# Forget gate of a two-layer hybrid trunk: the tokens' rows made stationary, the gate's 16 weight columns moving

## The chip, the cores and the metric

The kernel runs on one core of a Trainium2 chip, in one launch. The metric is the device time of that launch in microseconds. The kernel before takes 1617.2 us (median of three runs, 1616.39 to 1618.21).

## The reference, cut to what matters

Two request groups go through two layers with the same weights: one prompt of 512 tokens, and eight samples of 16 tokens with a history of 512. Together these are 640 rows of 1024 channels. A layer norms the rows, multiplies them by `w_in` (columns for retention, forgetting attention and a short convolution), mixes, multiplies by `w_out`, and then runs a gated feed-forward network. Eight columns of `w_in`, `fl`, are the forget gate's logits, one for each of the eight attention heads:

```python
h = _rms_norm(x, norm_mix)
proj = h @ w_in
rq, rk, rv, rg, fq, fk, fv, fl, cb, cc, ch = jnp.split(proj, split_at, axis=-1)
logf = jax.nn.log_sigmoid(fl.astype(f32) + fox_f_bias.astype(f32))
```

Everything is in 32-bit floats. `logf` is an output, and its running sum enters every attention score.

## The kernel before, in words

All 640 tokens are worked on together, as five tiles of 128 (the fifth holds the samples). The normed rows are turned, so that channels lie on partitions: `hhi` and `hlo` have shape [128, 8, 640]. Each float is split in two parts for TensorE's rounded format, the rounded value (`hi`) and the remainder (`lo`). ScalarE writes the first, VectorE the second. Weights come in slabs of 1024 columns per partition (`raw`), and are split in the same way into `whi` and `wlo`. A product is then three matmuls, hi by hi, hi by lo and lo by hi (`mm3`).

Every engine has its own program, written out by hand in the order in which it runs; semaphores join them. PSUM has eight banks; `plan_banks` lists the jobs of each bank in order, and a job waits until the one before it on its bank has been taken out (`wait_room`, `wait_taken`).

In a layer TensorE's order around the gate is this:

- the turning of the normed rows, between the first slabs of chunk 0 (chunk 0: the first 512 columns of `w_in`);
- the rest of chunk 0, then 24 small transposes of the convolution's taps (`rows`);
- the gate's product. Its eight weight columns have a hi and a lo part, side by side in `wfl` [128, 8, 2, 8], 16 columns for each of the eight groups of 128 channels. These 16 columns are the stationary side, and the tokens move, 320 at a time: 2 halves x 8 groups x (`hhi`, `hlo`) = 32 matmuls. The result has 16 rows (8 from the hi weights, 8 from the lo weights) and 640 columns, in two banks. ScalarE takes it to `flr` [16, 640] in two pieces;
- chunk 1, whose tile order is that of `CHUNK_PARTS`, with the turning of the rotated queries and keys (`rt`) in it, and two pieces of chunk 2;
- the gate's turning (`flT`): for each of the five token tiles one matmul with `flr` stationary and a constant `fsum` of eight columns moving. It turns the tile and adds its hi and lo rows. VectorE adds the bias and writes `lf`;
- the retention's scores (`rT`), states (`rv`, `kw`), outputs and, late in that stage, 64 small matmuls of the samples (`qw` by `s0`).

In the rows all matmuls of `mm` stand under L2156 and transposes under L2218, so they are told apart by the names of their tiles.

Of the kernel before, what the change touches and what calls it, by code (L numbers as in the profile page):

```python
# [30 lines left out]
F32 = mybir.dt.float32  # L31
# [3 lines left out]
ALU = mybir.AluOpType  # L35
# [40 lines left out]
CONST = {}  # L76
_at = 0
for _name, _n in (("ident", P), ("tri", 896), ("cs", TT * 64), ("kdec", TT * RH), ("qdec", 2 * P), ("g16", 2),
                  ("tris", P), ("bmask", 16), ("e0", P), ("bsel", NB), ("fsum", FH)):
    CONST[_name] = (_at, _n)  # L80
    _at += _n
NCONST = _at
# [2 lines left out]
def tables():  # L85

    p = np.arange(P)
    gamma = 1.0 - 2.0 ** (-5.0 - np.arange(RH))
    c = np.zeros((P, NCONST), np.float32)

    def put(name, a):
        o, n = CONST[name]
        c[:, o:o + n] = np.asarray(a).reshape(P, n)

    put("ident", np.eye(P))
    pos = np.stack([t * P + p for t in range(TP)] + [PAST + p % NS], 1)
    inv = np.float32(10000.0) ** (-np.arange(HD // 2, dtype=np.float32) / (HD // 2))
    ang = (pos.astype(np.float32)[:, :, None] * inv[None, None, :].astype(np.float32)).astype(np.float64)
    put("cs", np.stack([np.cos(ang), np.sin(ang)], 2))
    left = np.stack([SEQ - 1 - (t * P + p) for t in range(TP)] + [NS - 1 - p % NS], 1)  # L100
    put("kdec", gamma[None, None, :] ** left[:, :, None] * HD ** -0.5)
    par = p // HD
    put("qdec", np.stack([gamma[2 * hp + par][:, None] ** (p[None, :] % NS + 1) for hp in range(2)], 1))
    put("g16", np.stack([gamma[2 * hp + par] ** NS for hp in range(2)], 1))
    put("tri", (np.arange(896)[None, :] - 384) >= p[:, None])
    same = (p[:, None] // NS) == (p[None, :] // NS)
    put("tris", same & (p[:, None] <= p[None, :]))
    b8 = np.arange(NB)
    put("bmask", np.tile((p // NS)[:, None] == b8[None, :], (1, 2)))
    put("e0", (p[:, None] % FH) == (p[None, :] // NS))  # L110
    put("bsel", ((p % HD) // FH)[:, None] == b8[None, :])
    put("fsum", (p[:, None] < 2 * FH) & (p[:, None] % FH == np.arange(FH)[None, :]))

    dp = np.where(p[None, None, :] >= p[:, None, None],
                  gamma[None, :, None] ** np.maximum(p[None, None, :] - p[:, None, None], 0), 0.0)
    i = np.arange(P, SEQ)
    dq = np.stack([gamma[2 * hp + par][:, None] ** (i[None, :] - (SEQ - 1.0)) for hp in range(2)], 1)
    ds = np.where((same & (p[None, :] >= p[:, None]))[:, None, :],
                  gamma[None, :, None] ** np.maximum(p[None, None, :] - p[:, None, None], 0), 0.0)
    decay = np.concatenate([dp.reshape(P, -1) * HD ** -0.5, ds.reshape(P, -1) * HD ** -0.5, dq.reshape(P, -1)], 1)  # L120

    mb = np.zeros((P, P * (2 + NB)), np.float32)
    mb[:, 0:P] = np.eye(P)
    mb[:, P:2 * P] = np.where(p[None, :] <= p[:, None], 0.0, NEG)
    for b in range(NB):
        seen = (p[None, :] // NS == b) & (p[None, :] % NS <= p[:, None] % NS)
        mb[:, (2 + b) * P:(3 + b) * P] = np.where(seen, 0.0, NEG)
    return c, decay.astype(np.float32), mb
# [149 lines left out]
def plan_banks(banks):  # L278

    j = banks.job  # L280
    for t in range(TT):
        for g in range(2):
            j(("hT", 0, t, g), (2 * t + g) % 3)
    cb = chunk_banks()

    def chunk(c):
        for t in range(TT):
            j(("c", c, t), cb[c][t])

    def turns(name):  # L290
        for t in range(TT):
            j((name, t), TURN_BANKS[name][t])

    chunk(0)
    j("taps", 1)
    j(("fl", 0), 0)
    j(("fl", 1), 2)
    chunk(1)
    turns("rt")
    j("flT", 7)  # L300
    for par in range(2):
        j(("rs", 0, par), RET_S[0][par])
    j("rst", 4)
    for par in range(2):
        j(("rs", 1, par), RET_S[1][par])
    for hp in range(2):
        j(("rop", hp), hp)
    for hp in range(2):
        j(("ro", hp), 3 + hp)
    j("rss0", 1)  # L310
    j("rss1", 0)
    j("rds0", 1)
    j("rds1", 0)
    j("rso", 2)
    j("rsoT", 0)
    chunk(2)
    chunk(3)
    turns("qT")
    chunk(4)
    turns("kT")  # L320
    j("cs", 6)
    j("cc", 0)
    j("cn", 5)
    for k, own_banks in (("cc_", (7, 1, 2, 3)), ("ch_", (4, 6, 5, 0)), ("cb_", (2, 3, 2, 2))):
        for i in range(4):
            j((k, i // 2, i % 2), own_banks[i])
    for n, (hp, qbs) in enumerate(fox_units()):
        for par in range(2):
            j(("fs", n, par), FOX_S[n % 2][par])
        if n % 3 == 0 and hp < 3:  # L330
            j(("fo", hp), 1 + hp % 2)
    for n, (hp, qbs) in enumerate(fox_units()):
        for i in range(fox_banks_t(qbs)):
            j(("ft", n, i), FOX_T[i])
    for g in range(3):
        j(("orT", g), (4, 2, 6)[g])
    j(("fo", 3), 5)
    for n in range(STEPS):
        for key, b in batch_jobs(n):
            j(key, b)  # L340
    for n in range(2 * TT):
        j(("wo", n // TT, n % TT), n % 8)
    for t in range(TT):
        for g in range(2):
            j(("hT", 1, t, g), 4 + (2 * t + g) % 4)
    for i in range(4):
        j(("g", "pro", i // 2, i % 2), i)
    for i in range(4):
        j(("u", "pro", i // 2, i % 2), U_BANKS[i])
    banks.loop(PAIRS - 1, wino_jobs("g") + down_jobs() + wino_jobs("u"))  # L350
    for g in range(6):
        j(("last", g), LAST_BANKS[g])
    for key, b in end_jobs():
        j(key, b)
# [7 lines left out]
def build(nc, a):  # L362
    with ExitStack() as ctx:
# [40 lines left out]
        def K(name):  # L404
# [56 lines left out]
            [("upad", [P, 2, PADDED], F32), ("ccs", [P, 2, NTOK], F32)],  # L461
            [("t3h", [P, 4, HALF], F32R), ("t3l", [P, 4, HALF], F32R)],
            [("kbo", [P, 4, FW], F32)],
            [("flr", [2 * FH, NTOK], F32)],
            [("vm", [P, 2, 512], F32)],
            [("gnd", [P, TT * RH, HD], F32), ("gnsq", [P, TT * RH, HD], F32)],
            [("to_gnsq", [P, TT * RH * HD], F32), ("roT", [P, 2, SEQ], F32)],
# [130 lines left out]
        def mark(first, n, key):  # L598
            for s_ in range(first, first + n - 1):
                used_index[s_] = len(used_index)  # L600
            final[first + n - 1] = key

        mark(0, 4, ("c", 0, TT - 1))
        mark(FL, 2, ("fl", 1))
        for c in range(1, 5):
            mark(C0 + 4 * c, 4, ("c", c, TT - 1))
        for first, k in ((CC, "cc_"), (CH, "ch_"), (CB, "cb_")):
# [463 lines left out]
        def _(act):  # L1071
# [92 lines left out]
            for l in range(DEPTH):  # L1164
# [14 lines left out]
                upto(FL + 1, l)  # L1179
                evac("taps", taps[:, :, :], l, view=lambda b: b[:, 0:NCT * NTAP].rearrange("p (c n) -> p c n", c=NCT))  # L1180
                upto(C0 + 4, l)
                for half in range(2):
                    evac(("fl", half), flr[:, half * HALF:(half + 1) * HALF], l, view=lambda b: b[0:2 * FH, 0:HALF])
                upto(C0 + 6, l)

                def silu_tile(t):
# [263 lines left out]
        def _(dve):  # L1450
# [85 lines left out]
            for l in range(DEPTH):  # L1536
# [17 lines left out]
                for t in range(TT):  # L1554
# [22 lines left out]
                    if t in (0, 3):  # L1577
# [3 lines left out]
                upto(C0 + 9, l)  # L1581
                dve.wait_ge(dec_in, l * 48 + 48)
                dve.wait_ge(kw_ready, l * TT + TT)
                B.wait_full(dve, "flT", l)
                dve.wait_ge(foxg_in, l * 64 + 64)
                dve.tensor_tensor(lf[:, :, :], bank[B.bank("flT")][:, 0:40].rearrange("p (t h) -> p t h", t=TT),
                                  fbias[:, :].unsqueeze(1).to_broadcast([P, TT, FH]), ALU.add).then_inc(B.free[B.bank("flT")], 1)
                def masked_values(h):
                    if h == 2:
                        dve.wait_ge(vm_used, l * 2 + 1)  # L1590
# [560 lines left out]
        def _(pe):  # L2151
# [12 lines left out]
            def fill(ins, key):  # L2164

                ins.then_inc(B.full[B.bank(key)], 1)
# [93 lines left out]
            for l in range(DEPTH):  # L2260
# [29 lines left out]

                for i in range(2):
                    ready(FL + i, l)
                for half in range(2):
                    key = ("fl", half)
                    B.wait_room(pe, key, l)
                    ts = slice(half * HALF, half * HALF + HALF)
                    for k in range(KT):
                        for h_ in (hhi, hlo):
                            ins = mm(bank[B.bank(key)][0:2 * FH, 0:HALF], wfl[:, k, :, :].rearrange("p s n -> p (s n)"),
                                     h_[:, k, ts], k == 0 and h_ is hhi, k == KT - 1 and h_ is hlo)  # L2300
                        if half == 1 and k == 3:
                            ins.then_inc(slab_used, 1)
                    fill(ins, key)
                chunk(1, l, "rt", lambda t: pe.wait_ge(rot_ready, l * TT + t + 1))
                for half in range(2):
                    B.wait_taken(pe, ("fl", half), l)
                pieces = iter([(i, t) for i in range(3) for t in range(3)])

                def chunk2(i, tiles, l):
# [5 lines left out]

                for _ in range(2):
                    piece(l)
                B.wait_room(pe, "flT", l)
                for t in range(TT):
                    ins = mm(bank[B.bank("flT")][:, t * FH:(t + 1) * FH], flr[:, t * P:(t + 1) * P], K("fsum")[0:2 * FH, :], True, True)  # L2320
                fill(ins, "flT")


                B.wait_all_taken(pe, [("rt", t) for t in range(TT)] + [("c", 1, t) for t in range(TT)], l)

# [391 lines left out]
```

## Time and profile before

| what | value |
|---|---|
| median of three runs | 1617.2 us |
| profiled execution, device time | 1618.32 us |
| its span, first to last instruction | 1616.5 us |
| TensorE matmuls busy | 1595.0 us, 99% of the span, 10304 records |
| TensorE weight loads busy | 1389.9 us, 86% |
| VectorE busy | 1080.2 us, 67% |
| ScalarE busy | 687.2 us, 43% |
| GpSimd busy | 410.8 us, 25% |
| granted TensorE clock, mean | 0.999 |

The span lies within the device time of the same execution; 1.8 us lie around it. Busy shares are of the whole span. A matmul's recorded duration (some 0.39 us for 512 columns) holds its way through the array; successive ones overlap, so what a stream of them costs is the distance between their starts. A weight load (PEld) is a record of its own and overlaps the matmul ahead. The granted clock is 1.00 at 2.4 GHz and 0.50 at 1.2 GHz.

### The profile page before, as it was taken

The numbers are of one execution on the slowest core, as the hardware profiler recorded it, in microseconds if no ns is written. First come the engines' busy times: TensorE is split into PE (matmuls) and PEld (weight loads), VectorE is DVE, ScalarE is ACT, GpSimd is POOL, SyncE is SP. The second block draws the span as 40 slices with busy tenths as digits, with TensorE's granted clock in tenths as the row PEclk, the third lists the DMA queues.
The fourth block names the chain that finished last, engine by engine and source line by source line (L and its number), as shares of the span: only waits on it lengthen the run. The fifth ranks groups of instructions, "written<-read, shape, count | busy, mean of one in ns | idle before, by whom it ended". The sixth has DMA issues, their size and how long they took to land.

```text
span 1616.5 us, 29200 instructions
## 1 busy us (share of the span) xinstructions
PE 1595.0 (99%) x10304; PEld 1389.9 (86%) x10304; DVE 1080.2 (67%) x1749; ACT 687.2 (43%) x1285; POOL 410.8 (25%) x524
## 2 busy tenths in 40 slices
PE   7999999999999999999999999999999999999998
PEld 6878896688999999999888789867899999999997
DVE  4445447528977777777644553674399777777775
ACT  4224337416544444444433233463264444444442
POOL 1114200004433333333112140010044333333330
PEclk9999999999999999999999999999999999999999
DMA  8223423822222222222242224156213222222222
GB/s 247 79 50 87 137 85 105 301 78 66 79 78 78 85 83 81 90 89 78 72 110 66 70 80 144 66 178 227 85 60 105 85 87 88 78 78 78 78 78 71
DMA packets 125319, 160.04 MB, mean 99 GB/s; under 512 B 25636, under 2 KB 77294, under 8 KB 125166
## 3 DMA queue, kind: packets, MB, share of 16 engines
q1 hardware_dynamic: 125096, 158.65, 32.2%
q8 instruction: 50, 0.82, 0.2%
q10 hardware_dynamic: 144, 0.33, 0.1%
q14 instruction: 29, 0.24, 0.0%
HBM read 149.43 MB, written 9.53 MB: 98 GB/s over the span
## 4 chain that ended last, share of the span: by engine, by line
PE 94%; DVE 2%; ACT 1%; DVEq 1%; issue 1%; DMA 1%; POOL 0%; POOLq 0%; SPq 0%; ACTq 0%
PE bank L2156 89%; PE bank L2218 5%; DVEq L1837 1%; DVE pf L1840 1%; DMA raw<-in_w_in 0%; DVE xn L1505 0%; ACT pf L1284 0%; DMA raw<-in_w_gate 0%; DVE small L1827 0%; DVE hlo L1484 0%; DVE gulo L1484 0%; ACT xn L1152 0%; POOL small L923 0%; ACT hhi L1130 0%; POOLq L1046 0%
## 5 line engine op out<-in xcount | busy, mean ns | idle before, releaser
L2156 PE MATMUL bank<-whi,hhi 128*128 128x512 f32 x560 | 226.7, 405 | 2.4 <-ACT rso L1171 1.1
L2156 PE MATMUL bank<-whi,hlo 128*128 128x512 f32 x560 | 220.2, 393 | 0.0
L2156 PE MATMUL bank<-wlo,hhi 128*128 128x512 f32 x560 | 219.8, 393 | 0.0
L2156 PE MATMUL bank<-hhi,whi 128*128 128x320 f32 x640 | 199.2, 311 | 0.8 <-DVE hlo L1484 0.8
L2156 PE MATMUL bank<-hlo,whi 128*128 128x320 f32 x640 | 198.1, 310 | 0.0
L2156 PE MATMUL bank<-hhi,wlo 128*128 128x320 f32 x640 | 198.0, 309 | 0.0
L2156 PE MATMUL bank<-whi,guhi 128*128 128x512 f32 x440 | 174.1, 396 | 0.4 <-DVE gulo L1484 0.4
L2156 PE MATMUL bank<-wlo,guhi 128*128 128x512 f32 x440 | 173.8, 395 | 0.0
L2156 PE MATMUL bank<-whi,gulo 128*128 128x512 f32 x440 | 173.7, 395 | 0.0
L1460 DVE TENSOR_TENSOR wlo<-raw,whi 128x1024 fp32r<-128x1024 f32 x80 | 100.1, 1252 | 106.1 <-ACT whi L1079 104.8
L1943 DVE TENSOR_TENSOR x<-x,bank 128x512 f32<-128x512 f32 x220 | 143.1, 682 | 39.6 <-PE bank L2156 39.3
L2156 PEld LDWEIGHTS bank<-whi,hhi 128*128 128x128 f32 x560 | 106.1, 190 | 27.2 <-issue 4.6
L2156 PEld LDWEIGHTS bank<-whi,hlo 128*128 128x128 f32 x560 | 106.0, 189 | 23.1
L1079 ACT ACTIVATE whi<-raw 128x1024 fp32r<-128x1024 f32 x80 | 84.6, 1060 | 92.7 <-PE bank L2156 84.4
L2156 PEld LDWEIGHTS bank<-wlo,hhi 128*128 128x128 f32 x560 | 106.5, 190 | 19.9
L2156 PEld LDWEIGHTS bank<-hhi,whi 128*128 128x128 f32 x640 | 120.3, 188 | 2.5 <-issue 1.6
L2156 PEld LDWEIGHTS bank<-hlo,whi 128*128 128x128 f32 x640 | 120.3, 188 | 0.9
L2156 PEld LDWEIGHTS bank<-hhi,wlo 128*128 128x128 f32 x640 | 120.2, 188 | 0.0
L1044 POOL TENSOR_TENSOR s<-raw 128x512 f32<-128x512 f32 x60 | 90.1, 1502 | 83.6 <-DMA raw<-in_w_gate 83.6
L1044 POOL TENSOR_TENSOR s<-raw,gains 128x512 f32<-128x512 f32 x20 | 27.7, 1385 | 317.8 <-DMA raw<-in_w_up 227.7
L2156 PEld LDWEIGHTS bank<-whi,gulo 128*128 128x128 f32 x440 | 82.9, 188 | 19.3
L2156 PEld LDWEIGHTS bank<-whi,guhi 128*128 128x128 f32 x440 | 82.9, 188 | 19.3 <-DVE gulo L1484 1.0
(312 smaller groups left out, 3662.1 us busy)
## 6 DMA issues: line engine op xcount, KB each, us to landing
raw<-in_w_in SPq DMA_DIRECT2D x52, 512.0 KB, 3.7
raw<-in_w_gate SPq DMA_DIRECT2D x44, 512.0 KB, 3.8
raw<-in_w_down SPq DMA_DIRECT2D x44, 512.0 KB, 3.7
vb<-in_cache_fox_v SPq DMA_DIRECT2D x16, 1024.0 KB, 6.8
raw<-in_w_up SPq DMA_DIRECT2D x24, 512.0 KB, 3.8
gains<-in_w_up SPq DMA_DIRECT2D x20, 512.0 KB, 3.8
raw<-in_w_out SPq DMA_DIRECT2D x16, 512.0 KB, 4.8
kb<-in_cache_fox_k SPq DMA_DIRECT2D x8, 1024.0 KB, 6.7
```

The source lines that it names most:

```text
L1044: pool.tensor_tensor(by_k(out[:, :]), x_, y_, op).then_inc(s_sum, 1)
L1079: act.activation(whi[:, slot(n), 0:width(n)], raw[:, slot(n), 0:width(n)], ACT.Copy).then_inc(hi_split, 1)
L1460: dve.tensor_tensor(wlo[:, s_, 0:w_], raw[:, s_, 0:w_], whi[:, s_, 0:w_].bitcast(F32), ALU.subtract).then_inc(lo_split, 1)
L1837: dve.drain()
L1840: ins = dve.tensor_scalar(pf[:, m % 3, par, o:o + N], pf[:, m % 3, par, o:o + N], col(REC + fox_stat(m, i, par)), None, ALU.mult)
L1943: dve.tensor_tensor(x[:, t, 512 * c:512 * c + 512], x[:, t, 512 * c:512 * c + 512], bank[B.bank(key)][:, :], ALU.add).then_inc(B.free[B.ba ...
L2156: return pe.matmul(out, lhsT=lhsT, rhs=rhs, start=start, stop=stop, skip_group_check=True)
L2218: ins = pe.transpose(dst, src, ident[0:src.shape[0], 0:src.shape[0]])
```

## The change

The two sides of the gate's product are swapped. For each token tile, 128 tokens of `hhi` or `hlo` are stationary and the 16 columns of `wfl` move: 5 tiles x 8 groups x (`hhi`, `hlo`) = 80 matmuls. The result has the tokens on partitions, 5 x 16 columns in one bank. ScalarE takes it out in one piece. The five turning matmuls, their wait for both halves, their bank job and the constant `fsum` go; VectorE adds the hi and lo columns and then the bias.

```diff
-    j(("fl", 0), 0)
-    j(("fl", 1), 2)
+    j("fl", 0)
     chunk(1)
     turns("rt")
-    j("flT", 7)
...
-            [("flr", [2 * FH, NTOK], F32)],
+            [("flr", [P, TT, 2 * FH], F32)],
...
                 upto(C0 + 4, l)
-                for half in range(2):
-                    evac(("fl", half), flr[:, half * HALF:(half + 1) * HALF], l, view=lambda b: b[0:2 * FH, 0:HALF])
+                evac("fl", flr[:, :, :], l, view=lambda b: b[:, 0:TT * 2 * FH].rearrange("p (t n) -> p t n", t=TT))
                 upto(C0 + 6, l)
...
-                B.wait_full(dve, "flT", l)
+                B.wait_taken(dve, "fl", l)
                 dve.wait_ge(foxg_in, l * 64 + 64)
-                dve.tensor_tensor(lf[:, :, :], bank[B.bank("flT")][:, 0:40].rearrange("p (t h) -> p t h", t=TT),
-                                  fbias[:, :].unsqueeze(1).to_broadcast([P, TT, FH]), ALU.add).then_inc(B.free[B.bank("flT")], 1)
+                dve.tensor_tensor(lf[:, :, :], flr[:, :, 0:FH], flr[:, :, FH:], ALU.add)
+                dve.drain()
+                dve.tensor_tensor(lf[:, :, :], lf[:, :, :], fbias[:, :].unsqueeze(1).to_broadcast([P, TT, FH]), ALU.add)
...
-                for half in range(2):
-                    key = ("fl", half)
-                    B.wait_room(pe, key, l)
-                    ts = slice(half * HALF, half * HALF + HALF)
+                B.wait_room(pe, "fl", l)
+                for t in range(TT):
+                    ts = slice(t * P, (t + 1) * P)
                     for k in range(KT):
                         for h_ in (hhi, hlo):
-                            ins = mm(bank[B.bank(key)][0:2 * FH, 0:HALF], wfl[:, k, :, :].rearrange("p s n -> p (s n)"),
-                                     h_[:, k, ts], k == 0 and h_ is hhi, k == KT - 1 and h_ is hlo)
-                        if half == 1 and k == 3:
+                            ins = mm(bank[B.bank("fl")][:, t * 2 * FH:(t + 1) * 2 * FH], h_[:, k, ts],
+                                     wfl[:, k, :, :].rearrange("p s n -> p (s n)"), k == 0 and h_ is hhi, k == KT - 1 and h_ is hlo)
+                        if t == TT - 1 and k == 3:
                             ins.then_inc(slab_used, 1)
-                    fill(ins, key)
+                fill(ins, "fl")
                 chunk(1, l, "rt", lambda t: pe.wait_ge(rot_ready, l * TT + t + 1))
-                for half in range(2):
-                    B.wait_taken(pe, ("fl", half), l)
...
-                B.wait_room(pe, "flT", l)
-                for t in range(TT):
-                    ins = mm(bank[B.bank("flT")][:, t * FH:(t + 1) * FH], flr[:, t * P:(t + 1) * P], K("fsum")[0:2 * FH, :], True, True)
-                fill(ins, "flT")
```

On TensorE, in the first layer, from the taps' transposes to chunk 1: each row is a matmul, its bank, its moving and its stationary tile, and the shape of its result; the rows between are 28 more of the same pair, 14 into bank 0 and 14 into bank 2. Before:

```order
L2218 MATMUL bank1<-const_50,rows_116 128x19 x24
L2156 MATMUL bank0<-hhi_56,wfl_82 16x320
L2156 MATMUL bank0<-hlo_57,wfl_82 16x320
...
L2156 MATMUL bank2<-hhi_56,wfl_82 16x320
L2156 MATMUL bank2<-hlo_57,wfl_82 16x320
L2156 MATMUL bank1<-whi_53,hhi_56 128x512
```

And now, with 78 more of the pair's rows where the dots are:

```order
L2215 MATMUL bank1<-const_50,rows_116 128x19 x24
L2153 MATMUL bank0<-wfl_82,hhi_56 128x16
L2153 MATMUL bank0<-wfl_82,hlo_57 128x16
...
L2153 MATMUL bank1<-whi_53,hhi_56 128x512
L2153 MATMUL bank1<-wlo_54,hhi_56 128x512
```

Nothing else moved into or out of this place: the 32 matmuls have become 80, each with a 128-column weight load in place of a 16-column one, and chunk 1 follows as it did. The second place is behind the two pieces of chunk 2, ahead of the retention's scores. Before:

```order
L2156 MATMUL bank6<-wlo_54,hhi_56 128x512
L2156 MATMUL bank6<-whi_53,hlo_57 128x512
L2156 MATMUL bank7<-const_50,flr_139 128x8 x5
L2156 MATMUL bank0<-rT_97 128x128
L2156 MATMUL bank1<-rT_97 128x128
```

Now:

```order
L2153 MATMUL bank6<-whi_53,hhi_56 128x512
L2153 MATMUL bank6<-wlo_54,hhi_56 128x512
L2153 MATMUL bank6<-whi_53,hlo_57 128x512
L2153 MATMUL bank0<-rT_97 128x128
L2153 MATMUL bank1<-rT_97 128x128
```

The scores now follow chunk 2's pieces directly. On ScalarE, at the first place, what stands between the splits of the weight slabs (`whi`), before and then now:

```order
L1171 ACTIVATE taps<-bank 128x456
L1079 ACTIVATE whi<-raw 128x1024
L1171 ACTIVATE flr<-bank 16x320 x2
L1079 ACTIVATE whi<-raw 128x1024 x2
L1171 ACTIVATE rT<-bank 128x4x128
```

```order
L1168 ACTIVATE taps<-bank 128x456
L1076 ACTIVATE whi<-raw 128x1024
L1168 ACTIVATE flr<-bank 128x80
L1076 ACTIVATE whi<-raw 128x1024 x2
L1168 ACTIVATE rT<-bank 128x4x128
```

Two evacuations have become one; the two splits behind it still wait for it.

## Rows read from the trace of the kernel before

**Rows 1.** The page's chain that ended last: shares of the span by engine.

```profile
PE 94%; DVE 2%; ACT 1%; DVEq 1%; issue 1%; DMA 1%; POOL 0%; POOLq 0%; SPq 0%; ACTq 0%
```

**Rows 2.** TensorE's waits: who waited, for whom, us in total, times, longest.

```profile
PE bank L2218 <- DVE xn L1505: 11.0, 5, 9.1
PE bank L2156 <- DVE hlo L1484: 1.9, 3, 1.0
PE bank L2156 <- ACT rso L1171: 1.1, 2, 0.6
```

**Rows 3.** Timeline, TensorE, layer 1: start us, length us, stationary size, moving size, count.

```profile
45.83 1.65 PE L2218 MATMUL bank<-const,rows 19*128 19x19 f32 x24
47.41 0.32 PE L2156 MATMUL bank<-hhi,wfl 128*16 128x320 f32 x1
...
51.97 0.31 PE L2156 MATMUL bank<-hlo,wfl 128*16 128x320 f32 x1
52.12 0.40 PE L2156 MATMUL bank<-whi,hhi 128*128 128x512 f32 x1
```

**Rows 4.** The same, gate's turning, weight loads and matmuls.

```profile
84.58 1.19 PEld L2156 LDWEIGHTS bank<-const,flr 16*128 16x128 f32 x10 [0.35 <-issue]
84.58 1.28 PE L2156 MATMUL bank<-const,flr 16*128 16x8 f32 x10
85.79 1.16 PE L2156 MATMUL bank<-rT 64*128 64x128 f32 x16
```

**Rows 5.** Weight loads of tile flr, both layers: duration ns min/median/max.

```profile
L2156 PEld LDWEIGHTS bank<-const,flr x20: 180/187/188, 84.6 to 885.9; 16*128 16x128 f32 x20
```

**Rows 6.** Timeline, weight loads of 128 columns close behind each other.

```profile
189.78 0.19 PEld L2156 LDWEIGHTS bank<-tri,lcdl 128*128 128x128 f32 x1
189.89 0.30 PEld L2156 LDWEIGHTS bank<-const,lexp 128*128 128x128 f32 x2
190.11 0.19 PEld L2156 LDWEIGHTS bank<-hhi,whi 128*128 128x128 f32 x1
190.22 0.19 PEld L2156 LDWEIGHTS bank<-hlo,whi 128*128 128x128 f32 x1
```

**Rows 7.** Timeline, TensorE, layer 1, late retention stage.

```profile
108.82 2.04 PE L2156 MATMUL bank<-qw,s 64*64 64x16 f32 x64
111.44 0.47 PE L2156 MATMUL bank<-whi,hhi 128*128 128x512 f32 x1 [0.57 <-ACT rso L1171]
...
114.72 0.63 PE L2156 MATMUL bank<-whi,hlo 128*128 128x512 f32 x1
115.15 0.63 PE L2156 MATMUL bank<-whi,hhi 128*128 128x512 f32 x1
...
115.85 0.39 PE L2156 MATMUL bank<-whi,hlo 128*128 128x512 f32 x1
```

**Rows 8.** Windows: length, busy us (count) of PE PEld DVE ACT POOL, granted clock, DMA.

```profile
111.00:112.00 1.00, 0.56 (x3) 0.50 (x4) 1.00 (x2) 0.29 (x1) 0.00 (x0) 1.00 0.00 0
112.00:113.00 1.00, 1.00 (x4) 0.79 (x3) 0.86 (x2) 0.00 (x0) 0.00 (x0) 0.62 0.00 0
115.00:116.00 1.00, 1.00 (x4) 0.76 (x4) 1.00 (x2) 0.00 (x0) 0.00 (x0) 0.67 1.01 174
908.00:912.00 4.00, 3.43 (x77) 2.69 (x74) 0.74 (x2) 0.38 (x1) 0.00 (x0) 1.00 0.02 4
912.00:914.00 2.00, 2.00 (x11) 1.60 (x11) 1.86 (x4) 0.00 (x0) 0.00 (x0) 1.00 0.00 0
```

**Rows 9.** Timeline, TensorE, the program's start.

```profile
9.11 1.94 PE L2218 MATMUL bank<-const,xn 128*128 128x128 f32 x8 [9.11 <-DVE xn L1505]
12.09 0.79 PE L2156 MATMUL bank<-whi,hhi 128*128 128x512 f32 x1 [1.04 <-DVE hlo L1484]
...
16.52 0.47 PE L2156 MATMUL bank<-wlo,hhi 128*128 128x512 f32 x1
...
17.06 1.03 PE L2218 MATMUL bank<-const,xn 128*128 128x128 f32 x8
```

**Rows 10.** Timeline, ScalarE and VectorE around the gate, layer 1.

```profile
52.32 0.43 ACT L1171 ACTIVATE flr<-bank 16x320 f32<-16x320 f32 x1 [1.92 <-PE bank L2156]
52.65 1.99 ACT L1079 ACTIVATE whi<-raw 128x1024 fp32r<-128x1024 f32 x2
...
86.06 0.20 DVE L1586 TENSOR_TENSOR lf<-bank,fbias 128x40 f32<-128x40 f32 x1 [5.89 <-PE bank L2156]
```

More of the change, by code:

```diff
@@ L78 @@
 for _name, _n in (("ident", P), ("tri", 896), ("cs", TT * 64), ("kdec", TT * RH), ("qdec", 2 * P), ("g16", 2),
-                  ("tris", P), ("bmask", 16), ("e0", P), ("bsel", NB), ("fsum", FH)):
+                  ("tris", P), ("bmask", 16), ("e0", P), ("bsel", NB)):
     CONST[_name] = (_at, _n)
@@ L111, in tables @@
     put("bsel", ((p % HD) // FH)[:, None] == b8[None, :])
-    put("fsum", (p[:, None] < 2 * FH) & (p[:, None] % FH == np.arange(FH)[None, :]))
     dp = np.where(p[None, None, :] >= p[:, None, None],
@@ L603, in build @@
         mark(0, 4, ("c", 0, TT - 1))
-        mark(FL, 2, ("fl", 1))
+        mark(FL, 2, "fl")
         for c in range(1, 5):
```

## The prediction

> **What bounds the kernel now.** I began with the chain of waits: 94% of it is TensorE [rows 1]. TensorE's own list of waits then shows how little slack it has: 9.1 us before its first instruction, and after that only a few waits of a microsecond or less [rows 2]. So a microsecond added to TensorE's stream is a microsecond of the kernel, wherever it stands, and one taken away from it comes back. The timeline gives the two places that the change touches: the gate's product from 47.41 to 52.12 us [rows 3] and the gate's turning from 84.58 to 85.79 us [rows 4]. The second layer repeats both.
>
> **The stream as it is.** 32 matmuls of 320 columns start in 52.12 - 47.41 = 4.71 us, 0.147 us each [rows 3]. Their 16-column weight loads are hidden.
>
> **The stream as it will be.** 80 matmuls move 16 columns each, but each needs a load of 128 columns. No row shows just this pair. The nearest one is the turning that goes away: 128-column loads with 8 columns moving. Ten loads span 1.19 us, the last is 0.187 us long [rows 4, 5], so they start (1.19 - 0.187)/9 = 0.111 us apart; the ten matmuls, by the same sum without a row for the last one's length, come to about 0.114. Loads in the rounded format also start 0.11 us apart where the matmul between them is short [rows 6]. Upper bound: the whole turning over its ten loads, 1.21/10 = 0.121 us. Lower bound: the taps' transposes, whose loads are 128 columns wide as well and which take (47.41 - 45.83)/24 = 0.066 us each [rows 3]; they are transposes of 19 rows, an unlike operation, and I keep them for a rival. I take 0.1125 us: 80 x 0.1125 = 9.0 us, so +4.3 us a layer at the full clock (3.9 at 0.1075, 5.0 at 0.121).
>
> The Trainium skill, "TensorE: Matmul & The Clock Gate", section "Weight-path perf modes", says that fast weight load is given to 128-column weights unless they are FP32. By it no load here gets faster, and the sum stands; if the rule did not hold for the rounded format, the transposes' price would be the better one.
>
> **What goes.** The turning, from 84.58 to the next block's start at 85.79: -1.2 us a layer [rows 4]. The 0.35 us of issue ahead of it I count as staying, since the scores that now follow the 512-column matmuls need the same kind of change to a part of the array. Swapping ends there: +4.3 - 1.2 = +3.1 us a layer.
>
> **Edits that I cost at nothing.** ScalarE's one evacuation in place of two (0.43 us each, [rows 10]) starts when the product is full. The next tile on its bank is chunk 1's second, 6 matmuls or about 1.4 us behind; an evacuation of 80 columns started about 0.2 us after the product leaves that uncovered by nothing. Were it late, TensorE would wait for the rest of its 0.4 us. The two slab splits behind it started 0.5 us after the product's end and take 1.99 us; the slab that they feed first is wanted after 18 matmuls, 4.1 us, with one more pass of VectorE between: the distance is what it was. VectorE's extra add of 0.20 us falls in the 5.89 us for which it sat idle before `lf` [rows 10]; its wait is now met long before. Behind it stands the retention's masking, which waits for TensorE's scores in any case. No DMA and no queue is passed.
>
> **The clock.** This is the term that decides the size. The granted clock falls once in the whole trace, and it falls behind the one long run of matmuls that move just 16 columns: 64 of them from 108.82 us, a wait of 0.57 us, three full matmuls, then 0.62 in the window from 112 and back to 1.00 in the one from 115 [rows 7, 8]. In that time 512-column matmuls start 0.43 us apart (114.72 to 115.15) where they otherwise start 0.23 apart, which is the 1.2 GHz level. In the second layer the same sequence shows 1.00 throughout [rows 8], so that run was only just enough. The new product is also a run of 16-column matmuls, 9.0 us and not 2.0, and the taps' 1.6 us of 19-column transposes stand directly ahead of it. I expect the clock to fall inside it in both layers.
>
> What a weight load costs at the lower level can be read at the program's start, where matmuls are half as fast though the record of the clock shows no fall: eight transposes take 1.94 us there and 1.03 us at 17.06 [rows 9]. So I double the distance, to 0.22 us (0.212 by the ratio 0.43/0.227 of the big matmuls). In layer 1 of the trace the small run began at 108.82 and the clock fell at about 112.2, 3.4 us on. At 0.1125 us that is 30 of the new loads at full clock, and 50 at half: 50 x 0.1075 = +5.4 us. Then the lower level stays for a while: from 112.2 to 115.6 in [rows 7, 8], and through 4.4 us of dense work at the start, 12.09 to 16.52 [rows 9]. 3.4 us at half speed lose 1.7 us (4.4 would lose 2.2; a return soon after the product 0.4). Together +7.1 us a layer.
>
> Against this stands a rule. The Trainium skill, same page, section "HAM oscillation", ties the fall to gaps in which TensorE idles between bursts. By it the gapless product would keep its clock, and the kernel would be at the first rival's time. This trace does not agree in full: its fall has a gap of only 0.57 us in it.
>
> **The sum.** Per layer +4.3 - 1.2 + 5.4 + 1.7 = +10.2 us; two layers +20.4. The profiled execution's 1618.3 us would become 1638.7. It stands 1.1 above the median of the runs, so against the median: 1617.2 + 20.4 = 1637.6 us. Bounds of this case: 40 to 70 loads at half clock (4.3 to 7.5), 0.4 to 2.2 after, and one fall behind the `qw` run more or less (1.7 us in all): 1617.2 + 2 x (3.1 + 4.7) - 1.7 = 1631 to 1617.2 + 2 x (3.1 + 9.7) + 1.7 = 1645.
>
> **The rivals.**
> - *The clock holds.* Weight loads of the whole array may keep the level up, where the `qw` run's loads were 64 by 64; the second layer's `qw` run kept it, and so did the turning and the scores at 84.58. Then only the swap counts: 2 x 3.1 = 6.2 us, 1623.4 us (1622.6 to 1624.8 by the bounds of the load). Against it: the one fall there is, behind a shorter run.
> - *It falls in one layer only*, as with `qw`: 10.2 + 3.1, 1630.5 us.
> - *Not slower: the loads run at the taps' pace.* If a 128-column load with a narrow moving side starts every 0.066 us, the product takes 5.3 us, +0.6 - 1.2 = -0.6 us a layer, 1616.0 us in all. The product and the turning together are 4.71 + 1.21 = 5.92 us, so it decides below 5.92/80 = 0.074 us. For it: 24 rows of taps. Against it: ten of `flr` and the rounded format's loads at 0.11. By the skill's rule on FP32 it would not happen either.
> - *The whole product at half clock.* If the taps' transposes pull the clock down before the product begins: 80 x 0.1075 = 8.6, and 2.2 after, 3.1 + 10.8 = 13.9 a layer: 1645 us. The taps alone did not do it before.
>
> **How the numbers follow.** Falls in both layers 0.68, in one 0.08, clock holds 0.16, taps' pace 0.05, all at half clock 0.03. Forecast 1637.6 us. The range goes down to the second case, since without it more than 2 in 10 would be out: 1623 to 1645 us. A measurement of this kernel tells 0.2%, 3.2 us, from no change. Slower by more than that are all cases but the taps' pace: 0.93. Same: 0.05. Faster, 0.02, would need that pace and a saving in the turning's changeover too.
>
> **What would show it.** 160 matmuls `bank<-wfl,hhi` and `bank<-wfl,hlo`, 128*128 stationary and 128x16 moving, start 0.11 us apart at first and 0.21 to 0.22 from some point on; the granted clock shows about 0.50 from 2 to 5 us into the product until some microseconds into chunk 1; chunk 1 begins 4.3 us later than now if the clock holds, near 10 us later if it falls. The retention's scores follow 0.3 us behind chunk 2's matmuls, and VectorE no longer waits before `lf`. I am wrong if the clock stays at 1.00 through the product, if the distance at full clock is under 0.10 us, or if TensorE shows a new wait at chunk 1's second tile.

## The result, and the profile after

The changed kernel takes 1638.28 us (median of four runs, 1637.87 to 1641.84) against 1617.03 us for the kernel before (four runs; the 1617.2 us above are the median of its first three). The ratio is 1.0135, 95% interval 1.0123 to 1.0147. The forecast was 1637.6 us. The profiled execution took 1638.27 us with a span of 1636.5 us, 20.0 us more than before. In its rows all matmuls stand under L2153 and transposes under L2215.

The gate's product in the first layer, timeline of TensorE (start us, length us); it answers to [rows 3]:

```profile
45.32 1.66 PE L2215 MATMUL bank<-const,rows 19*128 19x19 f32 x24
46.91 0.28 PE L2153 MATMUL bank<-wfl,hhi 128*128 128x16 f32 x1
47.04 0.26 PE L2153 MATMUL bank<-wfl,hlo 128*128 128x16 f32 x1
...
50.06 0.26 PE L2153 MATMUL bank<-wfl,hhi 128*128 128x16 f32 x1
50.17 0.30 PE L2153 MATMUL bank<-wfl,hlo 128*128 128x16 f32 x1
50.32 0.36 PE L2153 MATMUL bank<-wfl,hhi 128*128 128x16 f32 x1
50.53 0.36 PE L2153 MATMUL bank<-wfl,hlo 128*128 128x16 f32 x1
...
60.77 0.36 PE L2153 MATMUL bank<-wfl,hlo 128*128 128x16 f32 x1
60.99 0.77 PE L2153 MATMUL bank<-whi,hhi 128*128 128x512 f32 x1
```

Up to 50.17 the starts are (50.06 - 47.04)/27 = 0.112 us apart, from 50.32 on (60.77 - 50.53)/48 = 0.213. The 80 matmuls take 60.99 - 46.91 = 14.08 us where the 32 took 4.71.

The second layer, the same view:

```profile
855.09 0.28 PE L2153 MATMUL bank<-wfl,hhi 128*128 128x16 f32 x1
...
855.67 0.26 PE L2153 MATMUL bank<-wfl,hlo 128*128 128x16 f32 x1
855.78 0.36 PE L2153 MATMUL bank<-wfl,hhi 128*128 128x16 f32 x1
855.99 0.36 PE L2153 MATMUL bank<-wfl,hlo 128*128 128x16 f32 x1
...
871.57 0.77 PE L2153 MATMUL bank<-whi,hhi 128*128 128x512 f32 x1
```

Here only six start at the short distance, and the product takes 16.48 us. The windows over both stretches (length, busy us and count of PE, PEld, DVE, ACT, POOL, granted clock, DMA share, GB/s):

```profile
46.90:50.30 3.40, 3.40 (x32) 3.39 (x31) 1.23 (x1) 1.50 (x2) 0.00 (x0) 0.99 0.02 5
50.30:61.00 10.70, 10.70 (x53) 10.70 (x52) 0.00 (x0) 0.00 (x0) 0.00 (x0) 0.50 0.17 49
61.00:63.80 2.80, 2.80 (x8) 2.22 (x9) 1.41 (x2) 2.13 (x3) 0.00 (x0) 0.50 0.00 0
855.10:855.80 0.70, 0.70 (x8) 0.70 (x7) 0.00 (x0) 0.60 (x2) 0.00 (x0) 0.99 0.00 0
855.80:871.50 15.70, 15.70 (x76) 15.70 (x76) 1.22 (x1) 0.89 (x1) 0.00 (x0) 0.50 0.12 34
871.60:876.20 4.60, 4.60 (x12) 3.63 (x13) 3.04 (x6) 2.13 (x3) 0.00 (x0) 0.50 0.15 26
117.00:122.00 5.00, 4.42 (x83) 3.59 (x80) 1.90 (x3) 0.38 (x1) 0.00 (x0) 1.00 0.00 0
```

The clock is at 0.50 from 50.3 to 63.8 us and from 855.8 to 876.2 us, 2.8 and 4.6 us into chunk 1. In both stretches PE and PEld are busy all the time: no gap precedes the fall. Busy here means that some matmul's record is open; it doesn't mean that columns move all the time. The last row is the stretch with the 64 small `qw` matmuls: the one fall that the kernel before had there [rows 8] is not in this execution.

The second place, TensorE, answers to [rows 4]: the turning is gone, and the scores start 0.36 us behind the last matmul of chunk 2's pieces.

```profile
94.48 0.39 PE L2153 MATMUL bank<-whi,hlo 128*128 128x512 f32 x1
94.84 1.16 PE L2153 MATMUL bank<-rT 64*128 64x128 f32 x16
```

ScalarE and VectorE, answering to [rows 10]; one evacuation of 0.24 us, and no wait of VectorE ahead of `lf`:

```profile
61.17 0.24 ACT L1168 ACTIVATE flr<-bank 128x80 f32<-128x80 f32 x1 [12.66 <-PE bank L2153]
```

```profile
90.33 0.19 DVE L1582 TENSOR_TENSOR lf<-flr 128x40 f32<-128x40 f32 x1
```

TensorE's waits are those of [rows 2], with nothing new among them:

```profile
PE bank L2215 <- DVE xn L1501: 10.4, 5, 8.7
PE bank L2153 <- DVE hlo L1480: 1.8, 3, 0.8
PE bank L2153 <- ACT rso L1168: 1.1, 2, 0.6
```

### The profile page after: what moved, and what is told of

Read it like the earlier page. It is cut to its first block, busy times and chain, and to the rows that moved or that the text cites. A ratio compares the mean times of both kernels' runs of the same rounds, so it can differ in the third digit from the quotient of the medians.

```text
span 1636.5 us, 29396 instructions
## 1 busy us (share of the span) xinstructions
PE 1615.8 (99%) x10380; PEld 1412.9 (86%) x10380; DVE 1081.2 (66%) x1751; ACT 685.1 (42%) x1283; POOL 410.2 (25%) x524
## 4 chain that ended last, share of the span: by engine, by line
PE 93%; DVE 3%; ACT 1%; DVEq 1%; DMA 1%; issue 1%; POOL 0%; POOLq 0%; SPq 0%; ACTq 0%
PE bank L2153 88%; PE bank L2215 5%; DVE pf L1837 1%; DVEq L1834 1%; DMA raw<-in_w_gate 0%; DMA raw<-in_w_in 0%; DVE xn L1501 0%; DVE hlo L1480 0%; ACT pf L1280 0%; DVE x L1940 0%; POOLq L1043 0%; POOL s L1041 0%; DVE small L1824 0%; DVE gulo L1480 0%; DVE wlo L1470 0%
## 5 line engine op out<-in xcount | busy, mean ns | idle before, releaser
L2153 PE MATMUL bank<-whi,hhi 128*128 128x512 f32 x560 | 227.2, 406 | 2.2 <-ACT rso L1168 1.1
L2153 PE MATMUL bank<-whi,hlo 128*128 128x512 f32 x560 | 220.6, 394 | 0.0
L2153 PE MATMUL bank<-wlo,hhi 128*128 128x512 f32 x560 | 220.5, 394 | 0.0
L2153 PE MATMUL bank<-hhi,whi 128*128 128x320 f32 x640 | 198.9, 311 | 1.0 <-DVE hlo L1480 1.0
L2153 PE MATMUL bank<-hlo,whi 128*128 128x320 f32 x640 | 197.8, 309 | 0.0
L2153 PE MATMUL bank<-hhi,wlo 128*128 128x320 f32 x640 | 197.7, 309 | 0.0
L2153 PE MATMUL bank<-whi,guhi 128*128 128x512 f32 x440 | 174.0, 395 | 0.4 <-DVE gulo L1480 0.4
L2153 PE MATMUL bank<-wlo,guhi 128*128 128x512 f32 x440 | 173.6, 395 | 0.0
L2153 PE MATMUL bank<-whi,gulo 128*128 128x512 f32 x440 | 173.6, 395 | 0.0
L2153 PEld LDWEIGHTS bank<-whi,hhi 128*128 128x128 f32 x560 | 106.7, 191 | 27.2 <-issue 4.6
L2153 PEld LDWEIGHTS bank<-whi,hlo 128*128 128x128 f32 x560 | 106.5, 190 | 23.2
L2153 PEld LDWEIGHTS bank<-wlo,hhi 128*128 128x128 f32 x560 | 106.9, 191 | 20.3
L2153 PEld LDWEIGHTS bank<-hhi,whi 128*128 128x128 f32 x640 | 120.1, 188 | 2.6 <-issue 1.8
L2153 PEld LDWEIGHTS bank<-hlo,whi 128*128 128x128 f32 x640 | 120.2, 188 | 0.9
L2153 PEld LDWEIGHTS bank<-hhi,wlo 128*128 128x128 f32 x640 | 120.1, 188 | 0.0
L2153 PEld LDWEIGHTS bank<-whi,gulo 128*128 128x128 f32 x440 | 82.8, 188 | 19.4
L2153 PEld LDWEIGHTS bank<-whi,guhi 128*128 128x128 f32 x440 | 82.8, 188 | 19.4 <-DVE gulo L1480 1.0
```

What stands on the lines that cost most here:

```text
L2153: return pe.matmul(out, lhsT=lhsT, rhs=rhs, start=start, stop=stop, skip_group_check=True)
```

## The experiments

All times are medians. Kernels e1 to e4 ran on one chip, where the kernel before takes 1617.08 us; e5 to e7 ran later on another, where it takes 1616.50 us. The ratios are against the kernel before on the same chip.

**e1: 128 columns move.**

```diff
-                            ins = mm(bank[B.bank("fl")][:, t * 2 * FH:(t + 1) * 2 * FH], h_[:, k, ts],
-                                     wfl[:, k, :, :].rearrange("p s n -> p (s n)"), ...)
+                            ins = mm(bank[B.bank("fl")][:, (t % 4) * P:(t % 4) * P + P], h_[:, k, ts],
+                                     wfl[:, :, :, :].rearrange("p k s n -> p (k s n)"), ...)
```

> The changed kernel, but each of the 80 matmuls moves all 128 columns of wfl in place of 16 (the gate's logits are then not computed; that part is left out). Theory A: the 128-column weight load sets the pace, and the clock fell because the product moves only 16 columns a matmul. 128 columns at full clock need 53 ns, less than the load's 0.111 us, so the distance stays at 0.11 us; the granted clock stays at 1.00; per layer 80 x 0.1115 = 8.9, less 4.7, less 1.2 for the turning: +3.0, in all 1617.0 + 6.0 = 1623 us. Theory B: a stream of back-to-back weight loads brings the clock down whatever moves: the clock falls as in the changed kernel, 1638 us. Theory C: the matmul, not the load, sets the pace: the distance grows by up to 47 ns, 80 x 0.047 x 2 = 7.5 us more than A, 1630 us.

Measured: 1637.48 us, ratio 1.0092 (1.0059 to 1.0125). The medians alone give 1.0126; the runs lie too far apart for either figure to say much. Five executions took 1639.18, 1621.8, 1637.48, 1638.06 and 1630.08 us, with a mean clock of 0.99, 1.0, 0.99, 0.99 and 0.995. TensorE in the profiled one (1639.18 us), first layer:

```profile
50.59 0.28 PE L2153 MATMUL bank<-wfl,hlo 128*128 128x128 f32 x1
50.71 0.31 PE L2153 MATMUL bank<-wfl,hhi 128*128 128x128 f32 x1
50.82 0.41 PE L2153 MATMUL bank<-wfl,hlo 128*128 128x128 f32 x1
51.03 0.42 PE L2153 MATMUL bank<-wfl,hhi 128*128 128x128 f32 x1
```

The distance is 0.11 us ahead of the fall (50.59 to 50.71), with eight times as much moving: the number of columns does not set it, and theory C falls. The clock fell all the same, so theory A, that it was the 16 columns, fails as I put it; theory B's 1638 us fits three of five executions, but not the one at 1621.8 us, whose mean clock was 1.0, nor the one at 1630.08 us. The first is the case "the clock holds" (A's 1623 us), and the second lies where a fall in one layer was put. The same kernel shows all three.

**e5: 256 columns move.** The same edit with `h_[:, k, 0:256]` as the moving side, made after e1's result.

> As e1_wide, but each of the 80 matmuls moves 256 columns of hhi or hlo (the gate's logits are left out). In the rows of before 256-column matmuls of this format start 0.115 us apart, as long as a weight load. Theory A': how much moves behind each load decides whether the clock holds; 16 columns lose it, 128 lose it mostly, 256 keep it: granted clock 1.00 in both layers, 80 x 0.115 = 9.2, less 4.7, less 1.2: 1617.0 + 6.6 = 1623.6 us. Rival B': back-to-back loads of 128 four-byte columns lose the clock whatever moves: 1638 us or more.

Measured: 1624.12 us (1623.48 to 1624.72), ratio 1.0046 (1.0031 to 1.0061). The windows over the product, first layer and second:

```profile
48.00:58.00 10.00, 10.00 (x86) 9.97 (x86) 1.23 (x1) 1.50 (x2) 0.00 (x0) 1.00 0.19 54
850.00:870.00 20.00, 20.00 (x133) 18.27 (x133) 9.17 (x16) 3.63 (x5) 2.14 (x2) 1.00 0.28 79
```

The 80 matmuls and their weight loads start 0.120 us apart (48.45 to 57.80 is 78 distances), nearly as dense as the 0.112 us of the changed kernel, and the clock holds in both layers. The product takes 9.7 us in each, +3.8 us a layer with the turning gone, which is the 7.6 us above the kernel before; 0.115 us a matmul had been expected. So dense loads alone do not take the clock down (rival B' falls), and the kernel that moves sixteen times as much is 14 us faster. With 16 columns the clock fell in both layers of the profiled execution and the four runs lie together; with 128 it fell mostly, with 256 in none of three. I draw no threshold from three points.

**e2: the product spread over chunk 0's last slab.**

```diff
-                chunk0(3, l)
-                ... the taps' transposes
                 for t in range(TT):
+                    chunk0(3, l, [t])
                     ... the 16 gate matmuls of token tile t
+                ... the taps' transposes
```

> The changed kernel, with the product's five token tiles (16 matmuls, 1.8 us each) placed one behind each token tile of chunk 0's last slab (6 matmuls of 512 columns, 1.4 us), so no instruction more or less. Theory A: it is the long unbroken run of 16-column matmuls that loses the clock; broken up by 512-column ones the clock holds, and only the weight loads remain: 1623 us. Rival: runs of 1.8 us are as long as the qw run of 2.0 us behind which the clock fell once in the kernel before, so it falls in some of them: 1625 to 1638 us.

Besides what is expected there, the taps' transposes change places with the product and now stand behind its last piece.

Measured: 1634.56 us, ratio 1.0109 (1.0094 to 1.0124), inside the rival's range but only in part for the rival's reason. TensorE in the first layer, the first gate tile with its neighbours, and what follows the last:

```profile
40.31 0.40 PE L2153 MATMUL bank<-whi,hlo 128*128 128x512 f32 x1
40.54 0.17 PE L2153 MATMUL bank<-wfl,hhi 128*128 128x16 f32 x1
40.57 0.26 PE L2153 MATMUL bank<-wfl,hlo 128*128 128x16 f32 x1
...
42.13 0.26 PE L2153 MATMUL bank<-wfl,hlo 128*128 128x16 f32 x1
42.24 0.48 PE L2153 MATMUL bank<-whi,hhi 128*128 128x512 f32 x1
42.56 0.39 PE L2153 MATMUL bank<-wlo,hhi 128*128 128x512 f32 x1
...
54.99 1.66 PE L2215 MATMUL bank<-const,rows 19*128 19x19 f32 x24
59.50 0.79 PE L2153 MATMUL bank<-whi,hhi 128*128 128x512 f32 x1 [2.85 <-DVE wlo L1456]
```

```profile
39.00:57.00 18.00, 17.58 (x134) 16.20 (x134) 0.00 (x0) 0.31 (x1) 0.00 (x0) 1.00 0.11 30
57.00:59.50 2.50, 0.00 (x0) 0.00 (x0) 1.28 (x2) 2.50 (x5) 0.00 (x0) 0.68 0.00 0
```

And in the second layer, timeline and windows:

```profile
862.69 0.26 PE L2153 MATMUL bank<-wfl,hlo 128*128 128x16 f32 x1
862.88 2.35 PE L2215 MATMUL bank<-const,rows 19*128 19x19 f32 x24
868.07 0.79 PE L2153 MATMUL bank<-whi,hhi 128*128 128x512 f32 x1 [2.85 <-DVE wlo L1456]
```

```profile
849.00:863.40 14.40, 14.40 (x109) 13.34 (x108) 0.00 (x0) 0.00 (x0) 0.00 (x0) 1.00 0.07 25
863.50:865.20 1.70, 1.70 (x17) 1.61 (x16) 0.00 (x0) 0.00 (x0) 0.00 (x0) 0.50 0.00 0
```

In both layers the whole product ran at 1.00. But moving it ahead of chunk 0's end took away what had covered the split of chunk 1's first slab: TensorE now waited 2.85 us for `wlo` in each layer, 5.7 us in all. The clock fell behind the product in both. In the first layer it fell inside the wait, which begins at 56.65. In the second it fell between 863.4 and 863.5, ahead of the wait and without a gap, some 0.6 us into the transposes, which took 2.35 us in place of 1.66. So the wait is not the whole cause: the last 16 gate matmuls and the 24 transposes now stand back to back, 3.4 us of narrow work. The wait was unforeseen and spoiled the time, but this execution shows that the product in pieces of 16, parted by 512-column matmuls, ran at 1.00.

**e6: the same, with the wait mended.** The taps' transposes go behind the first tile, and the 80 matmuls are cut 18, 19, 19, 24 behind the other four. So the transposes no longer touch a piece of the product.

```diff
-                chunk0(3, l)
+                chunk0(3, l, [0])
                 ... the taps' transposes
-                for t in range(TT):
-                    ... the 16 gate matmuls of token tile t
+                for t, n in ((1, 18), (2, 19), (3, 19), (4, 24)):
+                    chunk0(3, l, [t])
+                    ins = gate(n)
```

> As e2_spread, with its new wait mended: the taps' transposes stand behind the first tile of chunk 0's last slab, the 80 gate matmuls in pieces of 18, 19, 19 and 24 behind the other four tiles, so that no run of them is longer than 2.7 us and the last one covers the split of chunk 1's first slab. Nothing is left out. Theory A: the clock holds in both layers and TensorE shows no wait for wlo; only weight loads and the turning count, 80 x 0.1115 = 8.9, plus 0.1 for each of four changes to 512 columns, less 4.7, less 1.2: 1617.0 + 6.6 = 1623.6 us. Rival: a run of 2.7 us is enough for a fall, in one layer or both: 1626 to 1632 us.

Measured: 1622.36 us (1621.81 to 1623.97), ratio 1.0037 (1.0024 to 1.005); the expected terms add up to +6.8 us, not the +6.6 written. TensorE's waits name `wlo` no longer. The windows over the product, first layer and second:

```profile
38.00:60.00 22.00, 22.00 (x155) 19.65 (x154) 3.64 (x5) 3.97 (x6) 0.00 (x0) 1.00 0.21 65
845.00:870.00 25.00, 25.00 (x152) 22.16 (x151) 9.17 (x16) 3.19 (x4) 2.13 (x2) 1.00 0.22 64
```

The same 80 matmuls, the same results, the same evacuation, and 5.9 us above the kernel before on its chip, where the changed kernel was 21.3 us above its own runs of before: some 15 us are what the clock cost, and 5.9 us what the swap costs at full clock. Theory A holds for this order of work. Two things differ from the changed kernel, though: the long run is broken up, and the transposes no longer touch it. In all four kernels that lost the clock at this place (the changed one, e1, e2, e4) they do; in e5 they do as well, and it held. No run has 80 matmuls in one piece without the transposes beside them, so how much of the fall is theirs is not shown.

**e3: the turning alone.** The kernel before without the five turning matmuls; `lf` is made from a constant.

```diff
-                B.wait_room(pe, "flT", l)
-                for t in range(TT):
-                    ins = mm(bank[B.bank("flT")][:, t * FH:(t + 1) * FH], ...)
-                fill(ins, "flT")
...
-                B.wait_full(dve, "flT", l)
-                dve.tensor_tensor(lf[:, :, :], bank[B.bank("flT")][:, 0:40]...
+                dve.tensor_tensor(lf[:, :, :], K("cs")[:, 0:40]...
```

> The kernel before without the five turning matmuls a layer, VectorE adds the bias to a constant (the gate's logits are left out). It shows the second part of the change alone. By the prediction's term: -1.2 us a layer, 1617.0 - 2.4 = 1614.6 us. Rival: the retention's scores then come so early that they wait for ScalarE's evacuations of chunk 1, and nothing comes back: 1617.0 us.

Measured: 1615.02 us, ratio 0.9991 (0.9982 to 1.0), which is 2.1 us less than the median of before; the ratio's interval runs from no effect to 2.9 us. The timeline of TensorE settles what the times leave wide: the scores start 0.35 us behind the last 512-column matmul, with no wait for ScalarE.

```profile
83.53 0.39 PE L2154 MATMUL bank<-whi,hlo 128*128 128x512 f32 x1
83.88 1.16 PE L2154 MATMUL bank<-rT 64*128 64x128 f32 x16
```

**e4: two-byte weights.**

```diff
+                pe.wait_ge(masks_in, 16)
...
-                            ins = mm(bank[B.bank("fl")][:, t * 2 * FH:(t + 1) * 2 * FH], h_[:, k, ts],
-                                     wfl[:, k, :, :].rearrange("p s n -> p (s n)"), ...)
+                            ins = mm(bank[B.bank("fl")][:, t * 2 * FH:(t + 1) * 2 * FH], identb,
+                                     maskb[:, 16 * k:16 * k + 16], ...)
```

> The changed kernel with a bf16 tile of constants as the stationary side of the 80 matmuls and 16 of its columns moving (the gate's logits are left out): same count, same columns, but 2-byte weights. Theory A (the load of 4-byte weights sets the 0.111 us): the distance falls, towards 0.03 to 0.06 us, and the product takes 2.4 to 4.8 us; whether the clock falls in so short a run is open; about 1617.0 + 2 x (3.6 - 4.7 - 1.2) = 1612 us, up to 1619 with a fall in both layers. Rival: the distance is an issue cost of TensorE for any pair of load and matmul: it stays at 0.11 and the clock falls, 1638 us.

Measured: 1614.45 us, ratio 0.9987 (0.9977 to 0.9997). TensorE in the first layer, weight loads and matmuls; then a part of the second layer's block that lies at clock 1.00, and a part of the first's at 0.50:

```profile
47.18 2.15 PEld L2153 LDWEIGHTS bank<-maskb 128*128 128x128 bf16 x80
47.19 2.24 PE L2153 MATMUL bank<-maskb 128*128 128x16 bf16 x80
50.10 0.79 PE L2153 MATMUL bank<-whi,hhi 128*128 128x512 f32 x1 [0.67 <-DVE wlo L1456]
...
845.12 1.64 PE L2153 MATMUL bank<-maskb 128*128 128x16 bf16 x59
...
48.13 1.24 PE L2153 MATMUL bank<-maskb 128*128 128x16 bf16 x41
```

80 matmuls of the same count and columns span 2.24 us, 0.17 us of it the last one's own length: 0.026 us apart, less than a quarter of 0.112. All 80 loads are there, though the stationary tile is the same each time. So the rival, an issue cost of any pair, falls. Here both sides are bf16, so this run alone does not part the load from a fixed cost of a four-byte matmul; e2 does: where the load was hidden behind a 512-column matmul, the next gate matmul started 0.03 us later (40.54 to 40.57). Together they put the 0.112 us on the load of the four-byte weights. The clock fell around these too (0.71 over the window 47.0 to 49.5), 0.9 us into a block that the transposes precede without a gap, and in the second layer as well; yet the block is so short that the kernel stays below the one before.

**e7: the turning as transposes.** The kernel before, with its product. VectorE's add of the two parts and the bias becomes two operations (not shown).

```diff
-                for t in range(TT):
-                    ins = mm(bank[B.bank("flT")][:, t * FH:(t + 1) * FH], flr[:, t * P:(t + 1) * P], K("fsum")[0:2 * FH, :], True, True)
-                fill(ins, "flT")
+                transposes("flT", [(bank[B.bank("flT")][:, t * 2 * FH:(t + 1) * 2 * FH], flr[:, t * P:(t + 1) * P])
+                                   for t in range(TT)], l)
```

> The kernel before, its product unchanged, but the gate's turning done by five true transposes of 16 rows (identity, 16 columns out), with VectorE adding the hi and lo columns. Nothing is left out. The taps' transposes of 19 rows start 0.066 us apart, the ten records of the turning's matmuls 0.111: 5 x 0.066 + 0.2 for the changeover = 0.5 in place of 1.2 us, 2 x 0.7 = 1.4 us less: 1615.6 us, which would beat both kernels. Rival: TensorE then waits at the scores for ScalarE's last evacuations of chunk 1, and it is 1617 us.

Measured: 1615.39 us, ratio 0.9994 (0.9985 to 1.0003). The block is 84.26 - 83.85 = 0.41 us long where it was 1.21, and 0.41 against 1.20 in the second layer:

```profile
83.85 0.48 PE L2220 MATMUL bank<-const,flr 16*128 16x16 f32 x5
84.26 1.16 PE L2158 MATMUL bank<-rT 64*128 64x128 f32 x16
```

The profile shows 0.8 us a layer saved. The times put it 1.1 us ahead of the kernel before, but the interval holds 1: that it beats the kernel before is not shown by them.

## Why the prediction was right, point by point

*What bounds the kernel.* TensorE's stream, and it stayed so: no new wait, and its added time came through whole.

*The distance at full clock.* I took 0.1125 us from the ten loads of the turning; it is 0.112 us. 80 of them make 8.9 us, +4.2 us a layer where I wrote +4.3. e4 and e2 together show that the reason was right, the four-byte load. The lower bound of 0.1075 us that I used in the range came from no row.

*The turning.* -1.2 us a layer; e3 measured -2.1 us for two, with 0 to 2.9 us in its interval, and the gap of 0.35 us that I left standing did stay. With the distance it gives +3.0 us a layer, +6.0 in all; e6, at full clock, is 5.9 us above the kernel before.

*The edits at nothing.* The evacuation, the bank's next tile, the two splits and VectorE's extra add brought no wait. The cover that the product gives to the split behind it is real, though: e2 took it away and paid 2.85 us in each layer.

*The clock.* This was the step on which the size hung, and it held: a fall in both layers, behind a run of narrow matmuls, and e6 gives the time back. The cause was put too narrowly: I tied the fall to 16 moving columns, and e1 fell with 128. Its terms were off one by one. In the first layer the fall came 3.4 us into the product, as taken, with 5.2 us lost in it (14.08 - 8.9) and 1.4 behind (half of 2.8). In the second it came 0.7 us in, and cost 7.6 and 2.3: 74 loads at half clock, where my bounds were 40 to 70, and 2.3 us behind where they ended at 2.2. Together 16.5 us against 14.2 forecast. The fall behind `qw`, 1.7 us in the kernel before, did not occur in this execution, and TensorE started 0.4 us sooner. 2 x 3.0 + 16.5 - 1.7 - 0.4 = 20.4 us; the spans differ by 20.0. So the total lies nearer than its parts, and that is luck: a clock term 2.3 us short was set off by what I had put in the range as a fall more or less. That the 3.4 us taken from the one fall of before came true in the first layer is luck too: e1 fell 2.6 and 1.9 us into its product.

*The chances.* Those of the cases slower than 0.2% add up to 0.95, not 0.93; the slip does not touch the forecast.

*The rule on gaps.* The Trainium skill, "TensorE: Matmul & The Clock Gate", section "HAM oscillation", gave a kernel that keeps its clock. Both falls here came in gapless stretches, with PE and PEld busy throughout. The measurement decides: a long run of loads with little moving behind them lost the clock without any idling. That idling alone takes it down is shown by no run here: e2's fall in the first layer came in a wait, but behind 3.4 us of narrow work, and in its second layer the same work lost the clock ahead of the wait. The Trainium skill's rule on fast weight load, same page, section "Weight-path perf modes", agrees with the distances: the rounded format's four-byte loads stood 0.112 us apart, and the bf16 ones were four times as dense. The trace does not name the mode of a load.

*What stays open.* Why the fall comes 3.4 us into the product in one layer and 0.7 us in the other with the same instructions ahead of it, why e1 takes all three outcomes, what part the transposes ahead of the product have in the fall, and why one run of the changed kernel took 1641.84 us (mean clock 0.987 against 0.990). No kernel here was made to tell these.

## What to carry to other kernels

When a matmul's two sides are of unequal width, make the narrow one stationary: 32 loads of 16 columns hide behind 320 moving columns, while 80 loads of 128 columns stand bare at 0.112 us each, and the swap made product and turning 8.9 us long in place of 5.9 even at full clock. If a load-bound run can't be avoided, break it up with wide matmuls; the same work in pieces of at most 2.7 us, each between 512-column matmuls, held 2.4 GHz and was some 15 us faster. Count the small transposes beside a piece too: e4's block of 2.2 us lost the clock with 1.6 us of them ahead of it, and so did e2's last piece of 1.8 us with them behind it. The 2.7 us are no limit to rely on. When moving a block, ask what its length has been covering.

## What the runs showed of the hardware that I had not expected

- Loads of 128 bf16 columns with 16 columns moving go 0.026 us apart (80 in 2.24 us), four-byte ones 0.112 us.
- At the 1.2 GHz level the distance of the four-byte loads nearly doubles with the rest, 0.112 to 0.213 us (512-column matmuls: 0.23 to 0.43); a clock that falls in such a run costs as much as in a matmul-bound one. The distance of the bf16 pairs hardly moves: e4's rows give (1.64 - 0.17)/58 = 0.025 us at clock 1.00 and (1.24 - 0.17)/40 = 0.027 at 0.50.
- A small matmul right behind a 512-column one costs 0.03 us, since its load is hidden (40.54 to 40.57 in e2); the 512-column one behind the small run pays it back, 0.32 in place of 0.23 us.
- A kernel can sit on an edge: e1's executions, instruction for instruction the same, took 1621.8 to 1639.2 us by whether and where the clock fell.
